# A fused expert layer: the up product of a loop block with 512-column passes, its halves summed by VectorE

## What is computed

```python
a = jnp.einsum('td,tkd->tk', hb, peer_u[eb])      # up: token times expert vector
a = jax.nn.gelu(a, approximate=False)
return jnp.einsum('tk,tkd->td', (gb * a), peer_v[eb])   # down
```

## Time and profile before

| | |
|---|---|
| median of 3 runs | 1015.37 us (1015.36 to 1018.39) |
| the profiled execution | 1016.95 us, its span 1015.2 us |
| mean granted TensorE clock | 0.992 of full speed |
| busy, share of the span | PE 96%, PEld 88%, DVE 67%, ACT 43%, POOL 20% |
| chain that ended last | PE 91% (L1267 37%, L1566 34%), DVE 4%, DMA 2%, ACT 2% |

### The profile page before, as it was taken

The page is one execution under the profiler, slowest core; times in us unless marked ns, Lnnn a source line. Parts: engine busy times, 40 slices in busy tenths (PEclk is TensorE's granted clock), DMA queues, the critical chain, the costliest instruction groups (busy, mean ns, idle before and its releaser), DMA issues.

```text
span 1015.2 us, 18253 instructions
## 1 busy us (share of the span) xinstructions
PE 979.1 (96%) x6375; PEld 890.5 (88%) x6375; DVE 683.9 (67%) x1253; ACT 440.6 (43%) x697; POOL 200.4 (20%) x230
## 2 busy tenths in 40 slices
PE   4998799999999999999999999999999999999998
PEld 4987698888899978899999999999999999999997
DVE  4599663889889788656566665656566565656665
ACT  5443541311477744444444344444434444443442
POOL 2287502588588600000000000000000000000000
PEclk9998999999999999999999999999999999999999
DMA  6542223533512377555555555555555555555554
GB/s 199 172 132 83 83 84 125 193 95 99 160 53 79 104 230 237 189 204 173 199 184 188 195 178 205 168 204 178 194 193 179 203 170 205 174 198 187 185 197 154
DMA packets 69481, 168.34 MB, mean 166 GB/s; under 512 B 6692, under 2 KB 35384, under 8 KB 69448
## 3 DMA queue, kind: packets, MB, share of 16 engines
q1 hardware_dynamic: 69120, 167.83, 49.5%
q10 hardware_dynamic: 328, 0.08, 0.0%
HBM read 163.16 MB, written 4.72 MB: 165 GB/s over the span
## 4 chain that ended last, share of the span: by engine, by line
PE 91%; DVE 4%; DMA 2%; ACT 2%; issue 1%; SPq 0%; DVEq 0%; ACTq 0%
PE psum L1267 37%; PE psum L1566 34%; PE psum L1524 6%; PE psum L1438 5%; PE psum L1474 3%; PE psum L1531 2%; DVE big L782 2%; DMA raw<-in_peer_u_dram 1%; DMA big<-in_w_in_dram 1%; PE psum L1385 1%; PE psum L1468 1%; DVE big L803 0%; DVE big L799 0%; PE psum L1368 0%; PE psum L1332 0%
## 5 line engine op out<-in xcount | busy, mean ns | idle before, releaser
L1566 PE MATMUL psum<-rr 128*128 128x512 f32 x1536 | 369.3, 391 | 1.1 <-issue 0.7
L1267 PEld LDWEIGHTS psum<-h_all,rr 128*128 128x128 f32 x2688 | 332.6, 189 | 12.6 <-DVE big L839 4.2
L1267 PE MATMUL psum<-h_all,rr 128*128 128x256 f32 (+1 forms) x2688 | 335.6, 281 | 3.8 <-DVE big L839 3.8
L1566 PEld LDWEIGHTS psum<-rr 128*128 128x128 f32 x1536 | 280.7, 188 | 56.2 <-issue 0.9
L1037 DVE TENSOR_TENSOR rr<-raw,rr 128x1024 fp32r<-128x1024 f32 x109 | 133.5, 1225 | 216.9 <-ACT rr L652 216.9
L652 ACT ACTIVATE rr<-raw 128x1024 fp32r<-128x1024 f32 x109 | 115.6, 1061 | 296.4 <-PE psum L1566 296.4
L548 ACT ACTIVATE rr<-raw 128x1024 fp32r<-128x1024 f32 x108 | 114.6, 1061 | 45.4 <-DMA raw<-in_peer_u_dram 45.4
L976 DVE TENSOR_TENSOR rr<-raw,rr 128x1024 fp32r<-128x1024 f32 x108 | 131.6, 1219 | 0.1
L1267 PE MATMUL psum<-rr,h_all 128*128 128x256 f32 (+1 forms) x672 | 84.2, 288 | 7.7 <-DVE rr L698 4.6
L1267 PEld LDWEIGHTS psum<-rr,h_all 128*128 128x128 f32 (+1 forms) x672 | 80.9, 182 | 10.6 <-issue 6.9
L1023 DVE TENSOR_TENSOR rr<-psum,picks 128x2048 fp32r<-128x2048 f32 x32 | 72.4, 2289 | 9.4 <-PE psum L1524 7.7
(11 more groups left out here) (164 smaller groups left out, 735.9 us busy)
## 6 DMA issues: line engine op xcount, KB each, us to landing
raw<-in_peer_u_dram SPq DMA_DIRECT2D x128, 512.0 KB, 4.0
raw<-in_peer_v_dram SPq DMA_DIRECT2D x128, 512.0 KB, 3.6
big<-in_w_in_dram SPq DMA_DIRECT2D x10, 1024.0 KB, 5.8
big<-in_peer_wq_dram SPq DMA_DIRECT2D x8, 1024.0 KB, 5.7
big<-in_w_out_dram SPq DMA_DIRECT2D x4, 1024.0 KB, 5.3
up_kept<-gel SPq DMA_DIRECT2D x20, 128.0 KB, 3.7
gel<-up_kept SPq DMA_DIRECT2D x20, 128.0 KB, 3.5
big<-in_x_dram SPq DMA_DIRECT2D x2, 512.0 KB, 3.9
```

The source lines that it names most:

```text
L1267: i = pe.matmul(dst, lhs(a, k), rhs(b, k), start=(n == 0), stop=(n == 3 * DK - 1))
L1566: i = pe.matmul(psum[:, 4 + 2 * t + n, :], g_sp[:, s, x, t * P:(t + 1) * P], v_sp[s][:, y, n * 512:(n + 1) * 512], start=(first and m == 0 ...
```

## The change

The tokens get a second layout, `hx`, over the memory of `h_all`: for each slice k of the model width the 256 columns of the high part and then the 256 of the low part, side by side. `up` takes for each k one pass of 512 columns with the high part of the weights (the left half of the bank gathers high by high, the right half high by low) and one pass of 256 columns with the low part of the weights, which adds into the left half. VectorE then sums the two halves of the bank into `gel[s]` (`sum_halves`), with a reduction over pairs of elements that lie 256 columns apart, and ScalarE's Gelu works in place in `gel[s]`. The sum of block b + 1 stands in VectorE's order between block_g of block b and block_u of block b + 2. TensorE's wait ahead of up is for `d_sum` in place of `a_gel`. The early up products read the new layout with the same passes as before.

```diff
+        hx = h_all[:, :, :, :].rearrange("p b k t -> p (b k t)")[:, 0:DK * 2 * SEQ].rearrange("p (k b t) -> p k b t", k=DK, b=2)
...
             def block_g(s, b):
-                act.wait_ge(a_done, b + 1 - EARLY)
-                act.wait_ge(d_g32, b - 1)
-                act.activation(gel[:, s, :], psum[:, 2 * s, 0:SEQ], ACT.Gelu).then_inc(a_gel, 1)
+                act.wait_ge(d_sum, b + 1 - EARLY)
+                act.activation(gel[:, s, :], gel[:, s, :], ACT.Gelu).then_inc(a_gel, 1)
...
+            def sum_halves(s, b):
+                dve.wait_ge(a_done, b + 1 - EARLY)
+                dve.wait_ge(d_g32, b - 1)
+                dve.tensor_reduce(gel[:, s, :], psum[:, 2 * s, :].rearrange("p (b t) -> p t b", b=2), AX.X, ALU.add).then_inc(d_sum, 1)
...
                 block_v(s, b)
                 block_g(s, b, first)
+                sum_halves(1 - s, b + 1)
                 if not last:
                     block_u(s, b + 2)
...
+            sum_halves(0, EARLY)
             for b in range(EARLY, EARLY + 2):
                 expert_block(b % 2, b)
...
-                product(psum[:, 2 * s, 0:SEQ], lambda a, k: ut[s][:, a, k, :], lambda b, k: ht[:, b, k, :], a_done)
+                for k in range(DK):
+                    pe.matmul(psum[:, 2 * s, :], ut[s][:, 0, k, :], hx[:, k].rearrange("p b t -> p (b t)"), start=(k == 0), stop=False,
+                              skip_group_check=True)
+                    i = pe.matmul(psum[:, 2 * s, 0:SEQ], ut[s][:, 1, k, :], hx[:, k, 0, :], start=False, stop=(k == DK - 1),
+                                  skip_group_check=True)
+                i.then_inc(a_done, 1)
...
-                pe.wait_ge(a_gel, 2 * i + (1 - EARLY))
+                pe.wait_ge(d_sum, 2 * i + (1 - EARLY))
                 up(0, 2 * i + 2)
                 down(0, 2 * i, False, False)
```

More of the change, by code:

```diff
@@ L245, in layer @@
         ld_v3 = sem("ld_v3")
-        d_place, n_ev = sem("d_place"), sem("n_ev")
+        d_place, n_ev, d_sum = sem("d_place"), sem("n_ev"), sem("d_sum")
         d_rel, p_qk = sem("d_rel"), sem("p_qk")
@@ L586, in _ @@
                     act.wait_ge(p_t32, 1)
-                    act.activation(ht[:, 0], t32s, ACT.Copy).then_inc(a_hi, 1)
+                    act.activation(hx[:, :, 0, :], t32s, ACT.Copy).then_inc(a_hi, 1)
                 if h >= 2:
@@ L1188, in low_part @@
                 ks = slice(2 * n, 2 * n + 2)
-                pool.tensor_tensor(ht[:, 1, ks, :], t32s[:, ks, :], f(ht[:, 0, ks, :]), ALU.subtract).then_inc(p_hlo, 1)
+                pool.tensor_tensor(hx[:, ks, 1, :], t32s[:, ks, :], f(hx[:, ks, 0, :]), ALU.subtract).then_inc(p_hlo, 1)
             def staircase(dst, first_, second, done):
@@ L1530, in split_part @@
                     for a, b in ((0, 0), (0, 1), (1, 0)):
-                        i = pe.matmul(psum[:, early_bank(e), 0:SEQ], ut[0][:, a, k, :], ht[:, b, k, :],
+                        i = pe.matmul(psum[:, early_bank(e), 0:SEQ], ut[0][:, a, k, :], hx[:, k, b, :],
                                       start=(k == 0 and (a, b) == (0, 0)), stop=(k == DK - 1 and a == 1))
@@ L1578, in _ @@
                     up(1, EARLY + 1)
-            pe.wait_ge(a_gel, 1)
+            pe.wait_ge(d_sum, 1)
             up(0, EARLY + 2)
             down(0, EARLY, False, False)
-            pe.wait_ge(a_gel, 2)
+            pe.wait_ge(d_sum, 2)
             up(1, EARLY + 3)
@@ L1585, in _ @@
             with pe.Fori(EARLY // 2 + 1, NK // 2 - 1) as i:
-                pe.wait_ge(a_gel, 2 * i + (1 - EARLY))
+                pe.wait_ge(d_sum, 2 * i + (1 - EARLY))
                 up(0, 2 * i + 2)
                 down(0, 2 * i, False, False)
-                pe.wait_ge(a_gel, 2 * i + (2 - EARLY))
+                pe.wait_ge(d_sum, 2 * i + (2 - EARLY))
                 up(1, 2 * i + 3)
```

## The result

| | before | after |
|---|---|---|
| median of 6 runs | 1017.2 us | 1024.41 us |
| profiled execution's span | 1015.2 us | 1023.7 us |
| mean granted TensorE clock | 0.992 | 0.993 |
| block of the main loop | 5.560 us | 5.641 us |

The ratio is 1.0073 (95% interval 1.0057 to 1.0088): 7.4 us slower, where 5.8 slower was forecast. The block is the time from the first pass of up(22) to the first of up(127), over 105: before 416.22 to 1000.02, after 416.20 to 1008.52. 105 x 0.081 = 8.5 us is the whole difference of the two spans (1023.7 - 1015.2); the rest of the kernel, in sum, added nothing.

The account below looks back on a forecast made before the run. TensorE bounds the loop, VectorE's path close behind. A 0.60 move against 0.44 room, less TensorE's 0.05 gain, adds 0.055 a block, 5.8 us over 105: 1016.95 becomes 1022.7, median 1021; range 1011 to 1040 (forecast's own 1017 to 1027).

Parts of the forecast that it names:

- What bounds the loop: Main loop: TensorE's up and down products in turn, 5.56 us a block, with VectorE's path to the next up close behind.
- the room of 0.44: Between L976 (VectorE's low part of the u weights) and the up product: 0.61 - 0.17 = 0.44 us of possible delay.
- The sum at 0.69 us and its step at 0.60: VectorE's new reduction, priced by 512 elements read: 0.69 us long, moving L976 by 0.60.
- the price by what it writes: Lower bound for VectorE's sum, by 256 elements written: a move of 0.33, kernel 5 us faster; VectorE-not-late rival, chance 0.12.
- that of L971: Upper bound for VectorE's sum, by a stepped SBUF reduction: 1.02 us, a move of 0.93, +23 us; stepped-read rival, chance 0.26.
- The overrun is paid over two blocks: Main loop: a wait ahead of one up product delays the next; 0.105 us a block, block 5.615, 5.8 us in all.
- w: TensorE's wait ahead of each up product, forecast at 0.105 us.
- 2w: Two waits of TensorE ahead of up products together, forecast as 5.55 - 5.34 = 0.21 us.
- The equation: For TensorE's waits ahead of up: 2w = (move of L976) - 0.39, forecast at 0.21 us.
- The passes of up at 2.76, TensorE's block at 5.51: TensorE: 8 fewer passes take up from 2.81 to 2.76 us; with down at 2.75 a block of 5.51, gaining 0.05.
- the third rival: Up's passes don't get cheaper, up stays 2.81: block 5.64, +8 us, 1024; edge of the forecast's 0.58, no own chance.
- the law: Main loop: VectorE's move and TensorE's own block set 2w, half of it added per block; forecast 2w 0.21, block 5.615.

Follow-up runs that it names:

- the doses: Kernel before plus unneeded VectorE multiplications at the sum's place, of 256 elements, 512, or both (0.33, 0.60, 0.93 us of delay): ratios 1.0001, 1.0074, 1.0249.
- the run with both multiplications: Kernel before plus unneeded VectorE multiplications of 512 and 256 elements at the sum's place: ratio 1.0249, a block of 5.807 us.
- wide first: Changed kernel, up's 8 passes of 512 columns before its 8 of 256: 1.0071 (block 5.627) with the sum unmoved, 0.9952 (5.515) with it behind the low u weights.
- pairs: Changed kernel, sum behind the low part of the u weights, up's passes alternating two of 512 columns, two of 256: ratio 0.9950, block 5.508 us.
- turn_all_wide: Changed kernel, sum behind the low part of the u weights, up's low-weight passes also 512 columns wide (output wrong): block 6.347 us.

## Why the prediction was right

1. **What bounds the loop, and the room of 0.44.** Right, and shown by the doses. The 0.12 for weights that aren't loaded ahead measured 0.11 (338 for 227 ns).
2. **The sum at 0.69 us and its step at 0.60.** Measured 0.684 and 0.60. Neither the price by what it writes nor that of L971 applies. The stepped read of PSUM costs VectorE nothing here: it costs as much as L761's 512 elements in a row, 686. The Trainium skill (Advanced Engine Details and Errata, Memory Cachelines) has a penalty in SBUF for another line with each element, and L971 agrees (1.69 ns against 1.07); what it says of non-contiguous patterns in PSUM it says of matmuls, and it does not carry over to this read.
3. **The overrun is paid over two blocks.** Right in size (5.640 and 5.807 for 5.64 and 5.805). The form was not foreseen: the prediction let each up product wait w, and the trace has all of it at every other one: 0.365 + 0.10 = 0.47 us in the run with both multiplications, for a 2w of 0.49. The equation only fixes the sum of two waits.
4. **The passes of up at 2.76, TensorE's block at 5.51.** This step failed. Up takes 2.81, as the third rival had it, and down 0.036 more; where nothing holds TensorE up that is 5.593, and in the changed kernel 5.565. The wide passes step by 235 ns, and "something else than 225 to 229 ns" was one of the prediction's own signs of being wrong. The prediction priced each pass by its width alone, from rows in which passes of one width follow each other. The turn of widths, which is what the change made of them, was in no row but at the ends of up and down: the dear first passes of down stood in the trace of before, but hidden in the mean of 229.
5. **The sum.** Forecast 5.615, measured 5.641. With 5.593 on TensorE the law would give 2w = 0.60 + 4.95 - 5.42 = 0.13, a block of 5.66, which is too much. With the 5.565 that its passes sum to in the changed kernel 2w is 0.155 and the block 5.643. The same check on wide first, 5.534 on TensorE, gives 5.627, and 5.627 was measured. So TensorE's time was put 0.055 us too low (5.51 for 5.565), more than the gain of 0.05 that was claimed for it, and half of that, 0.027, came through to the block. That is why +5.8 stood near the measured +7.4: not because the passes were priced well, but because their price hardly counted. The prediction had said so ("TensorE's gain counts only half as long as VectorE sets the block"). Its third rival, with no gain on TensorE, a block of 5.64 and +8 us, was the closer one.
6. **What was costed at nothing** (Gelu from SBUF, the loads, the first and last blocks) was nothing: the loop holds all of the difference of the spans, and in it TensorE waits for L976 alone.

What the trace was to show was right for the sum, for L976 and for the releaser. It was wrong that the rows would show TensorE idle for about 0.1 at each up product and no longer fully busy, and that up would take 2.76.

The change's idea does pay: with the sum behind the low part of the u weights and the passes grouped by width, the kernel is 0.5% faster than before (0.9950 for pairs, 0.9952 for wide first, no difference between the two). Either edit alone does not: the sum alone moved is 1.0031, the passes alone grouped 1.0071.

## What to carry to other kernels

Idle time of an engine is room only at the place in its order where it lies; here 2.06 us of VectorE's idle time in each block stood ahead of the path, and the room on it was 0.44. When an instruction is added, put it behind the one that the bounding engine waits for, if its own reader allows that. And when passes are merged, keep passes of one width together and measure the step from start to start by position, not the mean of a group: the order that was best here is measured for these widths alone.

## What the runs showed of the hardware

- Passes of fp32r operands with 512 columns step by 227 ns when they follow each other without a break, with ScalarE, VectorE and the loads at work beside them (all 28 of a block in turn_all_wide). Behind passes of 256 columns they step by 231 to 241 ns with single ones at 224 and 228: two to five passes behind grouped narrow ones, ten behind an up product with the widths in turn. Wide passes behind a late start are dearer as well, with no narrow one near (233 231 233 231 229). Narrow ones step by 112 to 120. With the same columns, the order of the passes changes a block by 0.085 us (5.593 in turn, 5.515 wide first, 5.508 in pairs).
- Why is open: the bank and the choice of high or low weights are excluded, and the steps are the same to 1 ns from block to block. One rival no run tested is the rhythm of the weight loads: each has a row of 188 to 189 ns, longer than the step of a narrow pass and shorter than that of a wide one.
- VectorE's sum of 256 pairs, each 1024 bytes apart in PSUM, takes 684 ns, as much as 512 elements in a row; in SBUF a reduction with a step of 64 bytes costs 1.69 ns an element.
- A pass that is released late costs about 0.11 us beyond the wait itself, for the weights that could not be loaded ahead (a row of 0.50 for 0.40, a step of 338 ns for 227).
